# A three-block float32 model on one core: half of the expert weight loads issued by ScalarE

## The reference

```python
def ec_moe(h, w_router, w_gate, w_up, w_down):
    B, T, _ = h.shape
    cap = EC_FACTOR * T // N_EXPERTS
    aff = jax.nn.softmax((h @ w_router).astype(jnp.float32), axis=-1)
    wts, tok = lax.top_k(jnp.swapaxes(aff, 1, 2), cap)
    bidx = jnp.arange(B)[:, None, None]
    xs = h[bidx, tok]
    hid = jax.nn.silu(jnp.einsum('becd,edf->becf', xs, w_gate)) * jnp.einsum('becd,edf->becf', xs, w_up)
    y = jnp.einsum('becf,efd->becd', hid, w_down) * wts[..., None].astype(h.dtype)
    return jnp.zeros_like(h).at[bidx, tok].add(y)
```

## Time and profile before

| | |
|---|---|
| runs, us | 3551.9, 3554.92, 3556.33 (median 3554.92) |
| the profiled execution | 3554.84 us, span 3553.1 us |
| PE busy | 3238.5 us (91%) |
| PE weight loads, beside PE | 1859.7 us (52%) |
| DVE busy | 1517.0 us (43%) |
| ACT busy | 723.8 us (20%) |
| DMA | 588.36 MB, all of the kernel's own on one queue (q1) |
| mean granted PE clock | 0.968 of full speed |

### The profile page before, as it was taken

One profiled execution on the slowest core, in us unless ns is written; L12 is line 12 of the kernel. 1 busy time (PEld: TensorE's weight loads), 2 busy tenths in 40 slices (PEclk: granted clock), 3 DMA queues, 4 the chain that ended last, 5 costly groups with the idle time before them and its releaser, 6 DMA issues. The chain is left out here.

```text
span 3553.1 us, 39646 instructions
## 1 busy us (share of the span) xinstructions
PE 3238.5 (91%) x16518; PEld 1859.7 (52%) x16518; DVE 1517.0 (43%) x2332; ACT 723.8 (20%) x1110; POOL 0.2 (0%) x4
## 2 busy tenths in 40 slices
PE   7988989799897879999989898899998999999997
PEld 3476635344354533323232322687555886878874
DVE  2563146712296432222222221545443757475652
ACT  2210232311105410000000000100521332231403
POOL 0000000000000000000000000000000000000000
PEclk9998999899998989999999999999999999999998
DMA  7201033123211069999999999122211211221210
GB/s 257 95 3 64 32 108 136 48 95 131 82 48 55 25 255 428 427 428 428 427 428 428 427 428 414 70 72 89 76 48 48 71 66 54 72 72 48 72 47 24
DMA packets 120307, 588.36 MB, mean 166 GB/s; under 512 B 8897, under 2 KB 11073, under 8 KB 95425
## 3 DMA queue, kind: packets, MB, share of 16 engines
q1 hardware_dynamic: 120128, 585.83, 41.4%
HBM read 583.72 MB, written 2.10 MB: 165 GB/s over the span
## 5 line engine op out<-in xcount | busy, mean ns | idle before, releaser
L454 PE MATMUL ps<-hT,weight_ring 128*128 128x512 f32 x1216 | 544.3, 605 | 28.3 <-ACT hT L593 8.8
L454 PE MATMUL ps<-work,weight_ring 128*128 128x512 f32 (+1 forms) x960 | 426.9, 594 | 18.3 <-PEq L2675 8.3
L454 PEld LDWEIGHTS ps<-hT,weight_ring 128*128 128x128 f32 x1216 | 232.7, 194 | 316.8 <-issue 305.4
L454 PEld LDWEIGHTS ps<-work,weight_ring 128*128 128x128 f32 x960 | 182.0, 195 | 216.2 <-issue 205.5
L2248 PE MATMUL ps<-weight_ring,work 128*64 128x512 f32 x944 | 214.3, 597 | 32.3 <-DMA weight_ring<-in_w_up 19.7
L326 DVE TENSOR_TENSOR work<-work,ps 128x512 f32<-128x512 f32 x196 | 134.7, 687 | 248.7 <-PE ps L441 244.0
L441 PE MATMUL ps<-weight_ring 128*128 128x256 f32 x896 | 202.7, 379 | 0.0
L2378 DVE SCALAR_TENSOR_TENSOR xT<-ps,mod,xT 128x512 f32<-128x512 f32 x128 | 96.1, 751 | 224.4 <-PE ps L2266 222.0
L441 PE MATMUL ps<-hT,weight_ring 128*128 128x256 f32 x704 | 165.3, 392 | 19.5 <-DVE hT L602 15.6
L441 PEld LDWEIGHTS ps<-weight_ring 128*128 128x128 f32 x896 | 169.7, 190 | 24.7 <-issue 1.9
L2248 PE MATMUL ps<-work 128*64 128x512 f32 x672 | 153.3, 598 | 14.9 <-DMA work<-in_w_up 13.5
(11 more groups left out here) (395 smaller groups left out, 4206.7 us busy)
## 6 DMA issues: line engine op xcount, KB each, us to landing
weight_ring<-in_w_gate SPq DMA_DIRECT2D x34, 2048.0 KB, 40.3
weight_ring<-in_w_down SPq DMA_DIRECT2D x28, 2048.0 KB, 40.2
work<-in_w_up SPq DMA_DIRECT2D x27, 2048.0 KB, 38.9
weight_ring<-in_w_up SPq DMA_DIRECT2D x25, 2048.0 KB, 38.2
work<-in_w_down SPq DMA_DIRECT2D x21, 2048.0 KB, 40.3
weight_ring<-in_w_in_odd SPq DMA_DIRECT2D x20, 2048.0 KB, 7.8
weight_ring<-in_w_in SPq DMA_DIRECT2D x18, 2048.0 KB, 9.0
work<-in_w_gate SPq DMA_DIRECT2D x15, 2048.0 KB, 40.2
```

What stands on the lines that cost most here:

```text
L454: ins = pe.matmul(bank[0:m, 0:f], w[:, k, where:where + m], src[:, k, 0:ntok], start=k == 0, stop=k == kt - 1)
```

## The change

In the experts stage the set `by_scalar` holds the blocks of even number from 10 on. For these SP neither waits nor issues; it only counts the semaphore on. ACT issues them with `load_into(act, n)`, which loads block n + 9 for an odd n, at places of its program where it has waited for what frees block n: four behind the wait for the fourth gate product (from the second expert on; two in the first), two behind the wait for the eighth gate or up product, which stands behind the copies of the turned hidden rows. Sizes, slots, semaphores and PE's order stay as they are. (ACT's `after(down, 4 * e)` in front of the first pair is already true at that point, since PE does the gate products after the down products of the expert before.)

```diff
--- before.py
+++ after.py
@@ -151,6 +151,7 @@
         self.sum_order = {i: j for j, i in enumerate(summed)}
         self.h_parts = self.ring[:, 3, :].rearrange("p (q k t) -> p q k t", q=4, t=L)
         self.arrived = {}
+        self.by_scalar = set()
         self.issued = 0
         self.used = 0
 
@@ -206,12 +207,14 @@
                 continue
             sources, kt, c = self.plan[i]
             before = [j for j in range(i) if self.slot_of[j] == self.slot_of[i] and self.plan[j] is not None]
-            if before:
+            if before and i not in self.by_scalar:
                 sp.wait_ge(*self.free_at[before[-1]])
             sig = self.loaded[self.slot_of[i]]
             dst = self.block_view(i)
             for src, c0, n in sources:
-                if len(src.shape) == 2:
+                if i in self.by_scalar:
+                    pass
+                elif len(src.shape) == 2:
                     dst = self.slots[self.slot_of[i]][:, 0:kt * c]
                     sp.dma_start(dst, src).then_inc(sig.sem, 16)
                 else:
@@ -2198,6 +2201,16 @@
     def by_tile(a):
         return a.rearrange("p (t r) -> p r t", t=4)
 
+    slots = len(ch.slots)
+    ch.by_scalar = {first + n + slots for n in range(12 * E_ - slots) if n % 2 == 1}
+
+    def load_into(act, n):
+        i = first + n + slots
+        if i in ch.by_scalar:
+            (src, _, _), = ch.plan[i][0]
+            slot = ch.slot_of[i]
+            act.dma_start(ch.slots[slot][:, 0:SLOT], src).then_inc(ch.loaded[slot].sem, 16)
+
     with nc.Block() as block:
         @block.sync
         def _(sp):
@@ -2322,6 +2335,12 @@
             take_turned(0)
             for e in range(E_):
                 a.after(gate_up, 8 * e + 4)
+                if e > 0:
+                    a.after(down, 4 * e)
+                    load_into(act, 12 * e - 3)
+                    load_into(act, 12 * e - 1)
+                load_into(act, 12 * e + 1)
+                load_into(act, 12 * e + 3)
                 for p in range(2):
                     if e > 0:
                         a.after(hid_ready, 2 * e - 1 + p)
@@ -2337,6 +2356,8 @@
                     a(act.copy(hidT[:, p], ps[:, 6 - p, :].rearrange("p (t q c) -> p t q c", q=2, c=CAP)), hidT_ready)
                 if e + 1 < E_:
                     a.after(gate_up, 8 * e + 8)
+                    load_into(act, 12 * e + 5)
+                    load_into(act, 12 * e + 7)
                     take_turned(e + 1)
             for k in range(KD):
                 a.after(added, 8 * (E_ - 1) + k + 1)
```

## The result

The changed kernel takes 3570.53 us (median of 5 runs, 3567.52 to 3572.4) against 3552.21 us for the one before, measured beside it: ratio 1.0047, interval 1.0035 to 1.0058 (here and below the ratio and its 95% interval are taken over all executions of both kernels, so it is not quite the quotient of the medians). The profiled execution has a span of 3568.7 us, 15.6 more than before. Forecast were 3569 us, 3553 to 3593, and slower with a chance of 0.77.

The account below looks back on a forecast made before the run. The experts stage's DMA stream of 2 MB blocks was taken as the bound. The profiled 3554.84 us plus 13.7 for PE's later end, which includes 3.0 us of idle at the start, gave 3568.6, forecast as 3569 us, range 3553 to 3593.

Parts of the forecast that it names:

- The bound: Experts stage: the DMA stream sets the pace, 58.7 us per expert against PE's 52.5, once the nine-block lead is eaten.
- SP's lost issues and ACT's six new ones at 0: Experts stage: SP's six fewer issues gain nothing; ACT's issues, at most 0.53 us each, are hidden and cost 0.
- Idle at the start, 3.0 us: First expert: DMA idles 2.0 us before block 11 and 1.0 us before block 23, moving the last landing by 3.0 us.
- the second gap: First experts: DMA idle 1.0 us, since block 23 is issued at 1364.4 and earlier work lasts to 1363.4.
- The end, four blocks left at the last G: Expert 15: four blocks still to land when the fourth gate product ends (G), so PE ends 13.7 us later.
- likeliest case: Whole kernel: 3562 to 3576 us, chance 0.45, from end terms 8.8 and 18.6, 3.3 less if block 186 lands in time.
- Rival 1: Experts stage: ACT's blocks get half the DMA rate, making a 60.0 us cycle instead of 58.7; 3587 us, chance 0.17.
- Rival 2: Experts stage: two interleaved streams move less, 1% being 9 us and 2% 18; 3577 to 3587 us, chance 0.15.
- Rival 3: Experts stage: landing order follows need, lateness is hidden, only 3.0 us of idle count; 3558 us, chance 0.14.
- 4 (faster): Experts stage: a second queue fills gaps between blocks, at 433 GB/s with landings in order; 3548 us, chance 0.09.
- early periods: First experts' result copies: spaced some 55 us instead of 52.5, then 58 by the third expert.
- Large waits: PE in the experts stage: few waits for weights of 2 to 4 us at even blocks, gate 0 and up 2 above all.

Follow-up runs that it names:

- e7: The change plus six extra matmuls on PE before the wait for up block 2 in experts 1 to 15: 3570.74 us, ratio 1.0046 to the kernel before.
- e2: The change with ACT issuing each even block right behind the product that frees its slot, on both queues: 3555.84 us, ratio 1.0002 to the kernel before.
- e1: The change with SP issuing all blocks on one queue, even ones at the same late points: 3571.11 us, ratio 1.0048 to the kernel before.
- e5: The change with only the two latest blocks per expert on ACT, still late, ten on SP on time: 3598.60 us, ratio 1.0124 to the kernel before.
- e9: The change with the blocks in the slots of up 1 and up 3 issued later, behind the gathered-rows copy: 3572.43 us, ratio 1.0060 to the kernel before.
- e3: The change with the successors of down blocks 1 and 3 issued at once, the other four late: 3562.68 us, ratio 1.0020 to the kernel before.
- e4: The change with successors of gate and up blocks issued at once, those of down 1 and 3 late: 3571.63 us, ratio 1.0050 to the kernel before.
- e6: As e5, but SP issues the two late blocks too, at the same point on its one queue: 3571.80 us, ratio 1.0054 to the kernel before.
- e8: e5 plus six extra matmuls on PE before the wait for up block 2: 3560.15 us, ratio 1.0019 to the kernel before.

## Why the prediction was right, and where it was not

*The bound* was read rightly: the experts' stream of 2 MB blocks at 428 GB/s, PE ahead of it only by the lead of nine filled slots. e7 shows it best: the added work fills nearly all of PE's waits, and the time stays.

*SP's lost issues and ACT's six new ones at 0* holds: e2 has all of them and is at 1.0002. Single issues on ACT took up to 1.57 us, three times my bound, and were hidden.

*Idle at the start, 3.0 us.* The first gap is there. From 1307 to 1316 us before moves 328 GB/s; the change, from 1305 to 1315, moves 238, with a DMA share of 0.68:

```profile
1305.00:1315.00 10.00, 10.00 (x50) 3.42 (x48) 0.00 (x0) 0.00 (x0) 0.00 (x0) 1.00 0.68 238
...
1361.00:1364.00 3.00, 3.00 (x16) 0.77 (x12) 0.03 (x1) 0.00 (x0) 0.00 (x0) 1.00 0.90 377
```

The share leaves 3.2 us idle in the first row. Of these 1.9 stand before the first byte: 1.1 up to the first issue at 1306.08, and 0.8 from there on (before's stretch has 1.3 idle, 0.5 of it ahead of its issue at 1307.46). That leaves 1.3 for the 2.0 forecast. Of the second gap the 3 us at its place show 0.3 of 1.0.

*The end, four blocks left at the last G.* 3.6 were measured. G came at 2195.04, 20.1 us later than before counted from the stage's start, where 17.0 were forecast. From G to the end of the down products the change takes 34.8 us (2195.04 to 2229.83), before 39.2; forecast were 36.0. Up block 2 waited until G + 10.9, not 12. The 3.1 us by which G came later than forecast have two terms, of 2.1 and 1.0 us. The last load landed 5.1 us later than before, counted from the stage's start, and not 3.0: the idle time is 1.4 us shorter than forecast, but the stream at 426 in place of 428 GB/s makes some 4 us over 900. And that landing was at G + 20.6, not 21.6. It stood 14.2 us ahead of PE's end, where some 16 were forecast in place of 4. The errors cancel in part: 20.1 - 4.4 = 15.7 against 17.0 - 3.2 = 13.7, and the span shows 15.6.

*The number.* That the time itself was met within 2 us is partly luck: the forecast loss of 13.7 us was short of these 15.6, and of the 17 that the ratio gives, and the forecast started from an execution 2.6 us above the median that was measured beside the change. The bounds of its likeliest case, 3562 and 3576, do not follow from its terms, either: 8.8 and 18.6 give 3563.6 and 3573.4, and 3560.3 with the 3.3 taken off the lower.

*What failed is the cause given for that term:* "Two queues mean that odd blocks, issued early, land ahead of their turn". Odd blocks do land early, but e1 does the same with one queue and e2 has two queues without it. It is the late issue. The count at G was nearly right since it was made from times of issue, which did not ask how many queues there are.

*Rivals.* Rival 1, a cycle bound, did not decide in the change but does in e5, and its price there was not the half share alone: the half clock was 3 us of each cycle. Rival 2 is out: e2 moves 428 GB/s with both queues. Rival 3 (3558, all hidden) and 4 (faster) are out. The forecast that the early periods become some 55 and 58 was too smooth; they are 56.5, 61.2, 58.2, 60.5, and they follow the wait at up block 2: 6.27 us and a slow product in the third expert's 61.2, 2.27 us and a product of 3.65 in the 55.0 of the sixth. The later ones are 59.1 us on average, with 59.0 before. Large waits were forecast at gate 0 and up 2, of 2 to 4 us: they are all at up 2, of 2.0 to 6.3 us, and gate 0 has none over 1.1.

*What stays open:* how much of the loss the two latest blocks cause each, why the four others cost half of it alone and nothing beside them, and whether still more lateness of the up successors counts (e9). The half share of the two queues was not measured by itself; e5's second late block lands some 10 us after its first (24.2 and 14.5 us from their issues, 0.4 us apart), which is what half of the rate gives.

## What to carry to other kernels

Where a ring of buffers feeds a stream that is the bound, count at the last use how much of the stream is still to come: what has already landed but cannot be used yet is time lost, and the rate in the slices does not show it. A load may be moved to another engine's queue without harm as long as its issue stays at the event that frees its buffer; placing it behind a later wait of that engine costs a part of the lead. The block that is latest against its need has the largest part in the price, so mend that one first: e3 mended two of six and gained half, e4 mended the other four and gained nothing.

## What the runs showed of the hardware

Behind every wait at up block 2 of 3.8 to 6.9 us (the change, e1, e4, e5, e6, e9) the next product is slow: where the trace shows it by itself it takes 5.0 to 6.6 us instead of 3.65, and the granted clock is 0.53 to 0.61 in the stretches shown, between the levels of 2.4 and 1.2 GHz. Behind waits of 2.0 to 3.5 us it is so in some cases and not in others: in the change, two blocks behind a wait of 2.10 us took 8.78 us in place of 7.1, and one behind 2.27 us took 3.65; in e9 one behind 3.52 us took 3.65. This is free where PE is hidden (e7) and costs 37 us by the ratios where the same wait lies in PE's own cycle (e5 against e8), and there idle work in the wait removes it. I had not expected extra matmuls to make any kernel faster by 1%.

Loads of 2 MB from two queues move what those from one queue do: 428 GB/s from 1420 to 2180 us in e2_prompt and before. An issue on ACT took 0.33 to 1.57 us in the change.
